# A two-block transformer kernel: the context's modulation vector moves from the first MLP chunk into the second and third

## The reference, cut to what matters

```python
hid = jnp.square(jax.nn.relu(jnp.einsum('bsd,df->bsf', hn, w_up)))     # block 1
x = x + jnp.einsum('bsf,fd->bsd', hid, w_down)
...
mod_x = (jax.nn.silu(c) @ w_mod[l] + b_mod[l])[:, None, :]             # block 2
mod_c = jax.nn.silu(c_ctx) @ w_mod[l] + b_mod[l]
sh1, sc1, gt1, sh2, sc2, gt2 = jnp.split(mod_x, N_MOD, axis=-1)
csh1, csc1, cgt1, csh2, csc2, cgt2 = jnp.split(mod_c, N_MOD, axis=-1)
h_x = _modulate(x, g_pre_mix[l], sh1, sc1)
h_c = _modulate(ctx, g_pre_mix[l], csh1, csc1)
```

## Time and profile before

| | |
|---|---|
| median of 3 runs | 1307.11 us (1304.52 to 1311.71) |
| the profiled execution | 1308.12 us, its span 1306.3 us |
| busy, share of the span | PE 94%, DVE 52%, POOL 35%, ACT 33% |
| granted TensorE clock, mean | 0.971 of full speed |
| read from memory | 131.80 MB, 103 GB/s over the span |
| chain that ended last | PE 75%, DVE 17% (`mod_acc` L1725 4%), issue 3%, ACT 3% |
| `mod_acc` L1725, 112 of them | 131.9 us busy, mean 1206 ns |
| loads of `wm`, 48 of 512 KB | median 4.5 us from issue to landing |

### The profile page before, as it was taken

One profiled execution on the slowest core, in us unless ns is written; L12 is line 12 of the kernel. 1 busy time (PEld: TensorE's weight loads), 2 busy tenths in 40 slices (PEclk: granted clock), 3 DMA queues, 4 the chain that ended last, 5 costly groups with the idle time before them and its releaser, 6 DMA issues.

```text
span 1306.3 us, 17124 instructions
## 1 busy us (share of the span) xinstructions
PE 1228.6 (94%) x6252; PEld 1013.4 (78%) x6252; DVE 681.8 (52%) x971; ACT 430.6 (33%) x764; POOL 452.3 (35%) x188
## 2 busy tenths in 40 slices
PE   6799999889788999999988999999999999999997
PEld 4777777569566888888877887777798888888886
DVE  5565445535996875874366621785671131321315
ACT  5445432413311423323333210442442232241331
POOL 3422220203333545354453421210245435344340
PEclk9899999979888999999999999899999999999999
DMA  6322120202553665565333311302233223323211
GB/s 221 114 81 66 65 82 1 65 1 90 152 176 100 208 210 163 191 213 174 117 109 97 94 62 64 90 1 82 65 106 121 83 94 100 110 76 117 79 51 64
DMA packets 71157, 135.65 MB, mean 104 GB/s; under 512 B 6953, under 2 KB 9769, under 8 KB 71081
## 3 DMA queue, kind: packets, MB, share of 16 engines
q1 hardware_dynamic: 53730, 98.46, 24.2%
q10 hardware_dynamic: 17358, 36.27, 8.5%
HBM read 131.80 MB, written 2.13 MB: 103 GB/s over the span
## 4 chain that ended last, share of the span: by engine, by line
PE 75%; DVE 17%; issue 3%; ACT 3%; DMA 1%; POOL 1%; ACTq 0%; DVEq 0%
PE gemm L939 20%; PE gemm L941 20%; PE gemm L940 20%; DVE mod_acc L1725 4%; PE aux L1137 2%; DVE nmax L1840 1%; PE gemm L1170 1%; PE gemm L1171 1%; PE gemm L1172 1%; PE aux L1384 1%; DVE prob_t L1651 1%; DVE nmax L1555 1%; PE aux L980 1%; DVE xr L1445 1%; DVE gemm L1839 1%
## 5 line engine op out<-in xcount | busy, mean ns | idle before, releaser
L502 POOL TENSOR_TENSOR w_lo<-w_raw,w_hi 128x1024 fp32r<-128x1024 f32 (+1 forms) x180 | 447.1, 2504 | 817.0 <-ACT w_hi L721 456.8
L939 PE MATMUL gemm<-xt_hi,w_hi 128*128 128x512 f32 (+1 forms) x704 | 255.8, 363 | 5.0 <-issue 4.6
L940 PE MATMUL gemm<-xt_lo,w_hi 128*128 128x512 f32 (+1 forms) x704 | 254.8, 362 | 0.0
L941 PE MATMUL gemm<-xt_hi,w_lo 128*128 128x512 f32 (+1 forms) x704 | 254.8, 362 | 0.0
L939 PE MATMUL gemm<-w_hi,ht_hi 128*128 128x512 f32 x512 | 203.2, 397 | 6.3 <-POOL w_lo L502 6.3
L940 PE MATMUL gemm<-w_lo,ht_hi 128*128 128x512 f32 x512 | 201.7, 394 | 0.0
L941 PE MATMUL gemm<-w_hi,ht_lo 128*128 128x512 f32 x512 | 201.6, 394 | 0.0
L721 ACT ACTIVATE w_hi<-w_raw 128x1024 fp32r<-128x1024 f32 x124 | 125.5, 1050 | 207.6 <-PE gemm L941 113.6
L939 PEld LDWEIGHTS gemm<-xt_hi,w_hi 128*128 128x128 f32 x704 | 134.1, 190 | 26.6 <-issue 6.0
L941 PEld LDWEIGHTS gemm<-xt_hi,w_lo 128*128 128x128 f32 x704 | 133.8, 190 | 20.3
L940 PEld LDWEIGHTS gemm<-xt_lo,w_hi 128*128 128x128 f32 x704 | 133.9, 190 | 19.9
(11 more groups left out here) (215 smaller groups left out, 1535.2 us busy)
## 6 DMA issues: line engine op xcount, KB each, us to landing
wm<-in_w_mod ACTq DMA_DIRECT2D x48, 512.0 KB, 4.5
...
```

Of the source, the lines that this page charges most:

```text
L502: pool.tensor_tensor(w_lo[s % 2][:, ks, 0:width], raw[q][:, :, 0:width], w_hi[s % 2][:, ks, 0:width].bitcast(F32), ALU.subtract).then_inc( ...
L939: pe.matmul(bank, lh, rh, start=(k == 0), stop=False)
L940: pe.matmul(bank, lh, rl, start=False, stop=False)
L941: mm = pe.matmul(bank, ll, rh, start=False, stop=(k == KT - 1))
```

## The change

The context's vector is no longer made beside the other one in chunk 0. Every unit of `w_mod` is multiplied by one vector only. Chunk 0 keeps the four blocks of `mod_x` that it had. Chunks 1 and 2, the loop, do their four blocks of `mod_x` and then two blocks of the context each (`MC` = 2), for which the columns of `w_mod` are read again: 24 units in a chunk instead of 16, and 16 + 24 + 24 = 64 loads instead of 48. The number of multiply operations on DVE stays 128: 64, 32, 32 before and 32, 48, 48 after. The context's rows have a buffer of their own, `mod_row_c`, with its own load of the bias and its own store. The loop gets tables of its own; chunk 0 keeps the old ones.

```diff
-def vectors(i):
-    return 2 if isinstance(i, int) else 1
+def blocks(i):
+    return MB if isinstance(i, int) else MB + MC
...
                 if c >= 1:
-                    for u in range(mod_units(c - 2) + 2, min(mod_units(c - 1) + 2, MB_UNITS)):
-                        act.wait_ge(wm_used, before(i, 2 * MB_UNITS) + (GATE_CREDIT + 2 * vectors(i) * (u - 1)))
+                    for u in range(mod_units(c - 2, i) + 2, min(mod_units(c - 1, i) + 2, UQ * blocks(i))):
+                        act.wait_ge(wm_used, before(i, KT) + (GATE_CREDIT + 2 * (u - 1)))
                         wm_load(u, i)
...
-                src = t["w_mod"].rearrange("(u k p) n -> u p k n", k=UK, p=P)[
-                    u % 4, :, :, bass.ds(i * MB * NC + (u // 4) * NC, NC)]
+                k = u // UQ
+                col = i * MB * NC + k * NC if k < MB else i * (MC * NC) + (k - MB - MC) * NC
+                src = t["w_mod"].rearrange("(u k p) n -> u p k n", k=UK, p=P)[u % UQ, :, :, bass.ds(col, NC)]
                 act.dma_start(wm[u % 2][:], src).then_inc(wm_loaded[u % 2], 16)
...
-                pe.wait_ge(mod_split, before(i, MB) + vectors(i) * (k + 1))
+                pe.wait_ge(mod_split, before(i, 1) + (k + 1))
                 if k:
-                    pe.wait_ge(mod_rowed, before(i, MB) + vectors(i) * k)
-                for j in range(vectors(i)):
-                    pe.matmul(aux[j][0:1, :], ones_r[:], mod_hi[j][:], start=True, stop=False)
-                    mm = pe.matmul(aux[j][0:1, :], ones_r[:], mod_lo[j][k % 2][:], start=False, stop=True)
-                mm.then_inc(mod_summed, 1)
+                    pe.wait_ge(mod_rowed, before(i, 1) + k)
+                pe.matmul(aux[0][0:1, :], ones_r[:], mod_hi[:], start=True, stop=False)
+                pe.matmul(aux[0][0:1, :], ones_r[:], mod_lo[k % 2][:], start=False, stop=True).then_inc(mod_summed, 1)
...
-                acc = mod_acc[j][k % 2][:]
+                acc = mod_acc[k % 2][:]
                 w = wm[u % 2][:, row, :]
-                if e % (2 * nv) == 0:
-                    dve.wait_ge(wm_loaded[u % 2], i * (8 * MB_UNITS) + 16 * (u // 2 + 1))
+                c = csil[:, 0 if k < MB else 1, kt:kt + 1]
+                if row == 0:
+                    dve.wait_ge(wm_loaded[u % 2], before(i, 16 * UQ // 2) + 16 * (u // 2 + 1))
...
-MOD_SPLIT_IN = (5, 9, 12, 14)
-SUM_IN = (7, 11, 14, 15)
...
-MOD_DONE = (1, 2, 3, 4, 5, 6, 7, 8, 9, 11, 12, 14, 15, 16, 16, 16)
...
+def split_in(i):
+
+    return (5, 9, 12, 14) if isinstance(i, int) else (4, 6, 8, 10, 13, 14)
+
+
+def sum_in(i):
+
+    return (7, 11, 14, 15) if isinstance(i, int) else (5, 7, 9, 11, 14, 15)
+
+
+def mod_units(c, i):
...
+    if isinstance(i, int):
+        return (1, 2, 3, 4, 5, 6, 7, 8, 9, 11, 12, 14, 15, 16, 16, 16)[c]
+    return (1, 3, 5, 7, 8, 10, 12, 13, 15, 17, 19, 21, 23, 24, 24, 24)[c]
```

More of the change, by code:

```diff
@@ L99 @@
 MB = 12 * NC // ((NCH - 1) * NC)
-MB_UNITS = MB * UQ
+MC = 2 * D // NC // (NCH - 2)
 assert MB * NC == 2 * D
-def vectors(i):
-    return 2 if isinstance(i, int) else 1
+def blocks(i):
+    return MB if isinstance(i, int) else MB + MC
 def before(i, one):
-    return 0 if isinstance(i, int) else i * one + one
+    return 0 if isinstance(i, int) else i * ((MB + MC) * one) - MC * one
 EARLY = S // 2
@@ L264, in build @@
         wm = [at(f"wm{i}", [P, UK, NC], F32, A + 4 * K * i) for i in range(2)]
-        mod_lo = [[at(f"mod_lo{i}{j}", [P, NC], F32R, A + 8 * K + 4 * K * i + 2 * K * j) for j in range(2)]
-                  for i in range(2)]
-        mod_acc = [[at(f"mod_acc{i}{j}", [P, NC], F32, A + 8 * K + 4 * K * i + 2 * K * j) for j in range(2)]
-                   for i in range(2)]
+        mod_lo = [at(f"mod_lo{j}", [P, NC], F32R, A + 8 * K + 2 * K * j) for j in range(2)]
+        mod_acc = [at(f"mod_acc{j}", [P, NC], F32, A + 8 * K + 2 * K * j) for j in range(2)]
+        mod_row_c = at("mod_row_c", [1, MC, NC], F32, A + 12 * K)
         ct_hi = at("ct_hi", [P, KT, CTX], F32R, A)
@@ L748, in chunk @@
                     if mod:
[L749 removed]
+                        act.wait_ge(wm_used, before(i, KT) + GATE_CREDIT)
                         for u in range(2):
@@ L791, in mod_high @@
                 if k or not isinstance(i, int):
-                    act.wait_ge(mod_summed, i * MB + k)
-                for j in range(vectors(i)):
-                    act.activation(mod_hi[j][:], mod_acc[j][k % 2][:], ACT.Copy).then_inc(mod_hi_done, 1)
+                    act.wait_ge(mod_summed, before(i, 1) + k)
+                act.activation(mod_hi[:], mod_acc[k % 2][:], ACT.Copy).then_inc(mod_hi_done, 1)
             def wm_load(u, i):
-                src = t["w_mod"].rearrange("(u k p) n -> u p k n", k=UK, p=P)[
-                    u % 4, :, :, bass.ds(i * MB * NC + (u // 4) * NC, NC)]
+                k = u // UQ
@@ L1242, in chunk @@
                                (lambda: mid(c)) if mid is not None else
-                               (lambda: sum_mod(SUM_IN.index(c), i)) if mod and c in SUM_IN else None
+                               (lambda: sum_mod(sum_in(i).index(c), i)) if mod and c in sum_in(i) else None
                                ).then_inc(gemm_done, 1)
@@ L1726, in modulate @@
                 ins.then_inc(wm_used, 1)
             def split_mod(k, i):
-                dve.wait_ge(mod_hi_done, before(i, MB) + vectors(i) * (k + 1))
-                for j in range(vectors(i)):
-                    dve.tensor_tensor(mod_lo[j][k % 2][:], mod_acc[j][k % 2][:], mod_hi[j][:].bitcast(F32),
-                                      ALU.subtract).then_inc(mod_split, 1)
+                dve.wait_ge(mod_hi_done, before(i, 1) + (k + 1))
+                dve.tensor_tensor(mod_lo[k % 2][:], mod_acc[k % 2][:], mod_hi[:].bitcast(F32),
+                                  ALU.subtract).then_inc(mod_split, 1)
@@ L1735, in mod_rows @@
             def mod_rows(k, i):
                 if k == 0:
-                    dve.wait_ge(b_loaded, i * 16 + 16)
-                dve.wait_ge(mod_summed, i * MB + (k + 1))
-                for j in range(vectors(i))[::-1]:
-                    if j == 0 and vectors(i) > 1:
-                        dve.wait_ge(mod_rowed, before(i, MB) + (2 * k + 1))
-                    dve.tensor_tensor(mod_row[j][:, k, :], aux[j][0:1, :], b_row[:, k, :], ALU.add
-                                      ).then_inc(mod_rowed, 1)
+                    dve.wait_ge(b_loaded, i * 32 + 16)
@@ L1746, in norms_of_block_2 @@
+                dve.wait_ge(mod_summed, before(i, 1) + (k + 1))
+                row = mod_row[:, k, :] if k < MB else mod_row_c[:, k - MB, :]
+                dve.tensor_tensor(row, aux[0][0:1, :], row, ALU.add).then_inc(mod_rowed, 1)
             def norms_of_block_2(c):
```

66 lines of the change are left out of this document (33 added, 33 removed).

## The result

The changed kernel takes 1329.4 us in the median of four runs, the kernel before 1305.8 beside it: a ratio of 1.0171 between their means, 95% interval 1.0146 to 1.0196, so 19 to 26 us more; the medians differ by 23.5. The forecast was 1336.9 (29.8 slower), with a range of 1305 to 1352. The profiled execution took 1327.8 us, its span is 1326.0; before these were 1308.1 and 1306.3.

A forecast was written before the change was run, and what follows sets the result against it. PE's pace was the floor, with DVE holding up chunk 0 and two-buffer loads the changed loop. -21.2 us in chunk 0 plus 51.0 in chunks 1 and 2 gave +29.8, 1336.9 us against the median; range 1305 to 1352.

The forecast's parts named there:

- the three terms: Chunk 0 gains 21.2 us; chunks 1 and 2 lose 25.5 us each.
- Chunk 0, forecast a gain of 21.2: Chunk 0 loses half its modulation operations and ends at 398.5 instead of 419.7, with one 4.0 us stall at tile 8.
- The load round: Chunks 1 and 2: two buffers make two units take 6.6 us; POOL's blocking makes it 7.0 us a tile.
- floor 97.5: Chunks 1 and 2: by the loads, unit 23 is not consumed before 93 us, so no chunk ends before 97.5.
- would just fit: Chunks 1 and 2: by busy time alone, DVE's added operations fit, 90 us of work in 89.
- rival (a): Chunks 1 and 2: with sooner loads the loop holds PE's pace, about 90 us each, total 1288; chance 0.07.
- The wait in tile 5: Chunks 1 and 2: PE's first sum waits for DVE's split, a stall of 8.8 us, then fourteen slow matmuls.
- The waits after it: Chunks 1 and 2: PE waits for sums in tiles 9, 11 and 14, 2.2, 2.7 and 4.5 us.
- (b): Chunks 1 and 2: bound by loads alone at 3.3 us a unit, 97.5 us each, total 1303; chance 0.09.
- (c): Chunks 1 and 2: loads slow under their own traffic, 6 us to use, 126 us each, total 1361; chance 0.10.
- (d): Chunk 0 gains nothing, held by something other than DVE's operations; loop as forecast, total 1358; chance 0.02.

## Why the prediction was right, point by point

The sign, the two halves and their places came as forecast. The sum was +29.8 us; the stretches give +20.7 and the medians +23.5. Each of the three terms was off in the same direction, chunk 0's gain by 1.6 us and the two loop chunks by 4.1 and 3.3, so they did not cancel one another.

**Chunk 0, forecast a gain of 21.2.** Measured 22.8. One wait for `w_lo` at tile 8 (346.31), 3.1 us or a gap between matmuls of 3.5 where 4.0 stood, no wait for `mod_lo`. The slow stretch behind it came too, but with eight starts some 0.43 us apart and not fourteen. The sum had the right terms. (Chunk 0 ends at 393.0 us and not at 398 to 400, but 3.9 us of that are the earlier start.) The reading of the kernel before was a little high for the same reason: it took fourteen slow starts after each of the four waits, 11 us, and the trace has 12, 7, 13 and 14, some 9 us.

**The load round, forecast 6.6 us for two units and 7.0 with POOL.** Measured 7.2 in tiles 9 to 12. The two parts of it were separated: with POOL's operations halved the tile is 6.6 and 6.3 us and the chunks are 103.6 and 99.5 (floor 97.5); with a third buffer, which takes the wait for the loads away, they are 102.9 and 103.6. So the load round was sized right, and as a sum, 6.5 + 0.5, the period was too. But the sum hid that DVE's work with its blocking by POOL is a second limit beneath the first. A POOL operation that falls on DVE's wait for a load costs it little. In tile 9 of the changed kernel POOL's runs from 463.35 to 465.74, DVE waits until 465.10, and its two multiplications then take 1.97 us where two by themselves take 1.53. So DVE was busy 72.1 us there, and with the third buffer 82.5 for the same operations.

One side of the prediction did fail, though the forecast did not rest on it: the estimate that DVE's 90 us of work "would just fit", and rival (a), which said that a loop chunk would take about 90 if the loads came sooner. With a third buffer a load is asked for sooner, and the chunk took 102.9. Busy time was no bound here: DVE is idle for some 6 of the first 8 us of a chunk, waits for PE's banks later on (11.6 us in chunk 1 with three buffers and later sums), and its work has to be done in time tile by tile.

**The wait in tile 5, forecast 8.8 us and fourteen slow matmuls.** Measured 6.3 (gap 6.6), and some seven starts 0.43 us apart. This is where most of the excess of 4 us a chunk arises. Unit 0 was consumed 15.8 us after PE's start, not 17.0, and DVE's tiles 1 to 3 ended at 22.2, 27.5 and 34.2 instead of 23.6, 30.2 and 36.8. I had let each pair of units pay a round of 6.6 us. The pair of tile 2 took 5.3: its second load was issued at 415.46 and DVE used it at 419.30, 3.8 us later, where I had put 5.0 for all. The split was done at 36.3 and not at 38.8. From tile 6 on the measured times stay about 4 us ahead:

| end on DVE, us from PE's start | forecast | measured |
|---|---|---|
| tile 6 | 59.7 | 56.2 |
| tile 8 | 72.5 | 68.6 |
| tile 10 | 87.2 | 82.9 |
| tile 12 | 101.4 | 97.3 |
| unit 23 | 106.4 | 102.2 |
| PE's end | 114.4 | 110.4 |

**The waits after it.** In chunk 1 the gaps in tiles 9 and 11 are 1.9 and 2.6 us (forecast 2.2 and 2.7), and in tile 14 it is 4.7 (4.5) with its slow stretch, 2.6 us by the matmuls at 0.43 from 491.67 to 497.18 (2.8). One of 1.8 in tile 7 was not forecast. Chunk 2 differs in detail: its gap in tile 5 is 7.1 us and that in tile 14 only 2.6. The loop's granted clock is 0.94, where the prediction had about 0.93.

**The rivals.** (a) and (b) did not happen: the loop is far above 97. (c) did not either: the median landing is 4.7 us and was 4.6. The Trainium skill (DMA: Bandwidth & Descriptors, anatomy of one DMA) would put 512 KB at an estimate of 3.2 us, by a fit that it gives for DMAs issued by GpSimd. The loads here are issued by ACT's queue, beside those of the weights. The measured 4.7 us does not agree with the estimate, and the prediction went by its rows. (d) fell with chunk 0.

With POOL's operations halved, chunk 0 of before is 16 us shorter and the two loop chunks with three buffers 10.9 and 12.0. The prediction carried POOL with only 0.5 us per tile of the loop. The Trainium skill (SBUF — State Buffer, SBUF: two separate sides) has DVE and POOL exclude each other at a pair of ports that they share, and the loser wait for the whole operation. The rows at 466.59 and 455.27 agree with it; how much of each gain is this blocking and how much an earlier `w_lo` is taken up below.
